# A four-layer hybrid decoder step: four row groups at once, squares summed in pairs, and operations moved

## The chip, the cores and the metric

The kernel runs on all 8 cores of one Trainium2 chip. Every core works on its own sequence of the prompt (2048 positions) and on 16 of the 128 samples; the cores exchange nothing. The metric is the device time of the slowest core in microseconds (us). The engines are named as in the profile: PE (TensorE, matmuls), DVE (VectorE), ACT (ScalarE), POOL (GpSimd; here it issues the weight loads), SP (SyncE; it issues all other DMAs).

## What is computed

Four layers with width 1024, then a final RMSNorm. The parts that the change touches:

```python
h = _rmsnorm(x, norm1_g)
zb, zc, zv, zu, ga, gs = jnp.split(h @ w_in, cuts, axis=-1)
conv_out, new_buf = _conv_causal(zc * zv, conv_buf, conv_w, conv_b)
ya = zb * conv_out
ys, hr, hi = _s5(zu, h0_re, h0_im, ...)      # diagonal complex state space
gy = jax.nn.gelu(ys, approximate=False)
ys = gy * jax.nn.sigmoid(gy @ w_glu + b_glu)
m = jax.nn.sigmoid(ga) * (ya @ w_branch[:512]) + jax.nn.sigmoid(gs) * (ys @ w_branch[512:])
x = x + m @ w_out
h2 = _rmsnorm(x, norm2_g)
gate, up = jnp.split(h2 @ w_gate_up, [D_FF], axis=-1)   # D_FF = 2816
x = x + (jax.nn.silu(gate) * up) @ w_down
```

RMSNorm divides by sqrt(mean(x*x) + 1e-6) over the 1024 channels. The state of the S5 part is h_t = A h_{t-1} + B u_t with 64 complex states for each group of 16 channels. Outputs are the normed prompt and samples, and the new convolution and S5 states.

## The kernel before

**Tiles.** X (fp32) holds the residual as 8 row tiles of 128 channels; H (bf16) the normed input, R (bf16) 16 row tiles of intermediate results. The sequence is done in two halves of 1024 positions, each through all four layers: half 0 in two blocks of 512 columns, half 1 in three blocks of 384, 384 and 272 columns (the last holds 256 positions and the 16 samples). Weights come through RING, 6 slots of 128x2048 bf16, loaded by POOL in the order of use; done_unit frees a slot and issues the next load.

**The mixer.** It projects zu into R (rows UT), then goes over f, the four row tiles of the S5 channels. For each f: stage_b (B u for 8 positions at a time: 64 matmuls of 32 rows x 128 weight columns x 128 columns, weights WBF), conv_proj (32 matmuls for zc and zv into CIN), stage_a (the part of the output within 8 positions, weights KF, 12 matmuls of up to 512 columns), scan (on DVE: turn the states by TW, two scans, turn back, write HBF), stage_d (the part from the carried states, weights CAF, 64 matmuls of 32 weight columns x 128 columns in four column groups) with two Gelus on ACT, conv_rest (the convolution on ACT and DVE, and 16 matmuls for zb). Stage_b runs as two groups hf, with row groups hf and hf+2 in each: row groups 0 and 1 share PSUM bank 0, and 2 and 3 bank 1. Stage_a and stage_d share banks 2 and 3. The projections of the mixer use banks 4 to 7. After the loop come sigmoid gates of the merge (up to five in advance), the glu, the merge, w_out and the FFN.

**The norm.** norm_block squares the eight row tiles on ACT into H; a matmul of each with ONESB sums over the channels in PSUM (eight, accumulated). Ln and Exp on ACT give the scale, and eight operations on DVE write H (or, in the final norm, SCR slots that SP stores to yp). In half 0 the final norm also issues, row tile by row tile, the loads of half 1's X; X for block 0 of half 1's first norm is loaded apart (HX, the "held" block). The samples' x is loaded (xs) after the final norm.

**The start.** params() computes A and related figures of all layers into AB on DVE and ACT, and sends part of it through a DRAM buffer chd, to have it back in another layout. prep_g makes WBF, TW, BXB, CAF and KF of a layer; for layers after the first it runs in steps beside the FFN of the layer before.

**The order.** Nothing is issued in program order. Sched collects all operations with what they read and write (keys such as ("ps", bank) or "FFN0", written in the FFN) and finalize lays out each engine's queue: a list planner that simulates the engines with a cost for each operation, takes the ready operation with the lowest priority number (position in the program plus a bias: EVICT first, LATER for what may come late), and adds 1900 ns for a DMA to land; loads over 400,000 bytes share a pipe of 230 bytes per ns. The queues are fixed then, and on the chip each engine works through its own strictly in order. The change alters the planner's figures, so the order may differ anywhere.

## Time and profile before

| | us |
|---|---|
| three runs: lowest / median / highest | 3686.79 / 3977.66 / 4197.6 |
| the profiled execution | 3685.78 |
| its span (first to last instruction, slowest core) | 3684.0 |
| the other cores' spans | 3677.5 to 3682.5 |
| PE busy in the span | 3531.0 (96%) |
| DVE busy | 1969.2 (53%) |
| ACT busy | 1194.1 (32%) |

The busy time is from the profiled execution on the slowest core. Matmuls overlap in the profile: the cost of a group of matmuls is read from its start to the start of what comes next, not from the durations. "Granted clock" is TensorE's clock as a share of 2.4 GHz; it is at 1.2 GHz or 2.4 GHz, and a value between the two is a mean over the stretch.

### The profile page before, as it was taken

The page shows a single profiled execution, that of the slowest core. Times are in us where ns is not written, and L with a number is a line of the kernel's source. Part 1 is how long each engine was busy: PE and PEld are TensorE (multiplying, and loading weights), DVE is VectorE, ACT ScalarE, POOL GpSimd, SP SyncE. Part 2 cuts the span into 40 slices and gives each one's busy share as a digit, 9 for nine tenths or more (in the row PEclk, how much of TensorE's full clock was granted, in tenths as well). Part 3 has the DMA queues.
Part 4 walks back from the last instruction along what each step waited for, and adds up shares of the span by engine and source line. Part 5 has one row for each costly group of instructions (what it writes and reads, how often), then busy time and mean ns, then how long its engine had stood idle before and what let it go on. Part 6 is the DMA issues. An engine that isn't in the chain of part 4 may idle for free.

```text
span 3684.0 us, 65802 instructions; the slowest of 8 cores (3677.5 to 3684.0 us)
## 1 busy us (share of the span) xinstructions
PE 3531.0 (96%) x23936; PEld 1970.0 (53%) x23936; DVE 1969.2 (53%) x3510; ACT 1194.1 (32%) x2263; POOL 274.5 (7%) x531
## 2 busy tenths in 40 slices
PE   4799999999999999999979999999999999999998
PEld 1444444444444444444446666666666666666665
DVE  5847337472555627365355572655627456374323
ACT  4424223341334323242233332334323342233212
POOL 1000000000000000000000000000000000000000
PEclk9899999999999999999989999999999999999999
DMA  5244444344444434354454343344434444333343
GB/s 115 49 75 70 78 71 78 69 75 70 75 78 81 75 64 72 71 99 76 74 130 78 69 83 65 64 88 73 75 64 70 82 74 77 58 73 70 68 79 80
DMA packets 99530, 279.51 MB, mean 76 GB/s; under 512 B 14352, under 2 KB 25488, under 8 KB 99216
## 3 DMA queue, kind: packets, MB, share of 16 engines
q0 software_dynamic: 72576, 243.30, 38.7%
q1 hardware_dynamic: 26640, 32.00, 2.8%
q8 instruction: 200, 3.28, 0.4%
q14 instruction: 114, 0.93, 0.1%
HBM read 508.55 MB, written 9.98 MB: 141 GB/s over the span
## 4 chain that ended last, share of the span: by engine, by line
PE 90%; DMA 3%; issue 2%; DVE 2%; ACT 2%; SPq 1%; DVEq 0%; ACTq 0%
PE ps L401 90%; DMA PRS<-chd 1%; ACT SCR L405 1%; DVE R L412 1%; DMA X<-xp 1%; DMA GS<-cst 0%; SPq L390 0%; ACT L405 0%; ACT R L405 0%; DMA R<-xp 0%; SPq L384 0%; DVE PRS L412 0%; DMA CIN<-xp 0%; DVE SCR L418 0%; DVE H L418 0%
## 5 line engine op out<-in xcount | busy, mean ns | idle before, releaser
L401 PE MATMUL ps<-H,RING 128*128 128x512 bf16 (+2 forms) x12160 | 2184.0, 339 | 49.9 <-ACT SCR L405 17.6
L401 PEld LDWEIGHTS ps<-H,RING 128*128 128x128 bf16 x12160 | 1181.1, 98 | 991.0 <-issue 83.3
L401 PE MATMUL ps<-R,RING 128*128 128x512 bf16 (+2 forms) x6400 | 1184.2, 338 | 4.9 <-ACT SCR L405 3.2
L405 ACT ACTIVATE SCR<-ps 128x384 f32<-128x384 f32 (+2 forms) x824 | 419.8, 514 | 1580.4 <-PE ps L401 1508.0
L401 PEld LDWEIGHTS ps<-R,RING 128*128 128x128 bf16 x6400 | 621.5, 98 | 495.4 <-issue 15.5
L412 DVE TENSOR_TENSOR R<-SCR,ps 128x272 bf16<-128x272 f32 (+2 forms) x520 | 296.2, 582 | 602.9 <-PE ps L401 563.6
L452 POOL DMA_DIRECT2D RING<-wseq x504 | 266.2, 528 | 3365.7 <-PE ps L401 3241.1
L412 DVE TENSOR_TENSOR X<-X,ps 128x512 f32<-128x512 f32 (+2 forms) x480 | 280.2, 584 | 406.3 <-PE ps L401 403.5
L412 DVE TENSOR_TENSOR SCR<-SCR,ps 128x512 f32<-128x512 f32 (+2 forms) x304 | 173.9, 581 | 261.2 <-PE ps L401 228.6
L405 ACT ACTIVATE H<-X 128x512 bf16<-128x512 f32 (+2 forms) x352 | 189.0, 543 | 287.1 <-DVE X L412 273.6
L412 DVE TENSOR_TENSOR PRS<-PRS 128x256 f32<-128x256 f32 (+2 forms) x391 | 194.0, 505 | 81.5 <-DMA PRS<-chd 56.9
L418 DVE SCALAR_TENSOR_TENSOR H<-X,PT,SCR 128x512 bf16<-128x512 f32 (+2 forms) x312 | 182.3, 644 | 25.5 <-ACT SCR L405 25.4
L401 PE MATMUL ps<-H,ONESB 128*128 128x384 bf16 (+2 forms) x360 | 117.0, 351 | 55.4 <-ACT H L405 53.5
L405 ACT ACT_TABLE_LOAD x67 | 86.0, 1283 | 138.7 <-PE ps L401 85.4
L405 ACT ACTIVATE R<-ps 128x512 bf16<-128x512 f32 (+5 forms) x164 | 79.1, 544 | 80.1 <-PE ps L401 79.8
L405 ACT ACTIVATE WBF<-PRS,MG 128x512 bf16<-128x512 f32 x128 | 92.1, 719 | 36.8 <-DVE PRS L412 32.2
L412 DVE TENSOR_TENSOR CIN<-ps,SCR 128x512 f32<-128x512 f32 (+2 forms) x80 | 46.7, 584 | 103.7 <-PE ps L401 103.7
L405 ACT ACTIVATE CAF<-PRS 64x512 bf16<-64x512 f32 x112 | 70.4, 629 | 97.8 <-DVE PRS L412 92.7
L412 DVE TENSOR_TENSOR R<-SCR 128x384 bf16<-128x384 f32 (+2 forms) x152 | 89.0, 586 | 14.0 <-DVE SCR L412 1.4
L401 PEld LDWEIGHTS ps<-H,ONESB 128*128 128x128 bf16 x360 | 34.3, 98 | 102.5 <-issue 83.7
L401 PE MATMUL ps<-R,WBF 32*128 32x128 bf16 (+1 forms) x2176 | 74.6, 217 | 14.7 <-DVE PRS L412 8.4
L412 DVE TENSOR_TENSOR PRS<-TW 128x16 f32<-128x16 f32 (+6 forms) x196 | 84.6, 460 | 7.6 <-issue 0.2
(90 smaller groups left out, 1266.6 us busy)
## 6 DMA issues: line engine op xcount, KB each, us to landing
RING<-wseq POOLq DMA_DIRECT2D x376, 512.0 KB, 6.1
RING<-wseq POOLq DMA_DIRECT2D x64, 384.0 KB, 4.8
RING<-wseq POOLq DMA_DIRECT2D x64, 320.0 KB, 4.1
X<-xp SPq DMA_DIRECT2D x8, 512.0 KB
PRS<-chd SPq DMA_DIRECT2D x32, 128.0 KB
yp<-SCR SPq DMA_DIRECT2D x16, 256.0 KB, 10.3
yp<-SCR SPq DMA_DIRECT2D x16, 192.0 KB, 2.0
GS<-bst SPq DMA_DIRECT2D x8, 256.0 KB
```

The lines of the kernel that those rows point to most:

```text
L401: return S.op("pe", lambda e: e.matmul(out, lhsT=lhsT, rhs=rhs, start=start, stop=stop, **kw), reads=reads, writes=writes, mode=pmode(lhsT ...
L405: return S.op("act", lambda e: e.activation(out=out, in_=in_, func=func, **kw), reads=reads, writes=writes, cost=180.0 + 0.83 * numel(out) ...
L412: return vop(lambda e: e.tensor_tensor(out=out, in0=a, in1=b, op=op), out, reads, writes, bias)
L418: return vop(lambda e: e.scalar_tensor_tensor(out=out, in0=a, scalar=s, in1=b, op0=op0, op1=op1), out, reads, writes, bias, 1.1)
L452: S.op("pool", lambda e: e.dma_start(out=RING[:, slot, 0:n], in_=wseq[l, :, o:o + n]), writes=[("w", slot)], deps=deps, dma_sem=f"w{slot}" ...
```

## The change

- Half 0: stage_b4 takes the place of stage_b, with all four row groups in one group of 64 matmuls, each row group in a bank of its own (banks 0 to 3, columns 0 to 255).
- Half 0: stage_y takes the place of stage_a and stage_d. It uses columns 256 to 511 of banks 0 to 3, and runs one tile later: stage_y(f-1) after scan(f), stage_y(3) at the end.
- Half 0, all norms but the first of layer 0 and the final one: the squares of row tiles 0 and 1, 2 and 3, 4 and 5 go to SCR in fp32, DVE adds the two into H, and PE sums five tiles.
- The final norm of half 0: the stores of a block come after all its loads of X; the second block's results go to R and not to SCR.
- x_sample is loaded at the start into unused columns of X, and copied by ACT where it was loaded before. The last loads of X (384 columns) wait for the norm of half 1's last block.
- The negation of C in prep_g waits for AB; the copies and products of sample_loads wait for FFN0. The first layer's KF uses banks 6 and 7.
- The planner: a DMA lands after 3500 ns, loads over 100,000 bytes share a pipe of 260 bytes per ns; tiled matmuls cost 0.108 ns a column (0.216 with two row groups at work).

```diff
+NPAIR = (0, 2, 4)
...
-                if o.nbytes > 400000:
-                    pipe = max(pipe, end) + o.nbytes / 230.0
+                if o.nbytes > 100000:
+                    pipe = max(pipe, end) + o.nbytes / 260.0
                     end = pipe
-                end += 1900.0
+                end += 3500.0
...
-        cost = max(26.0, n * 0.23) if "tile_position" in kw else max(36.0, n / 2.4 + 1.0)
+        cost = max(7.0, n * (0.216 if two else 0.108)) if "tile_position" in kw else max(36.0, n / 2.4 + 1.0)
...
-        ts(stc[:, 1, :], stc[:, 1, :], -1.0, None, ALU.mult, ALU.bypass, kC + ["FFN0"], kC)
+        ts(stc[:, 1, :], stc[:, 1, :], -1.0, None, ALU.mult, ALU.bypass, kC + ["FFN0", "AB"], kC)
...
-            b = 2 + f % 2 if PF["first"] else 7
+            b = 6 + f % 2 if PF["first"] else 7
...
-        act(SSTB[:], SST[:], AF.Copy, ["SST"], ["SSTB"])
+        act(SSTB[:], SST[:], AF.Copy, ["SST", "FFN0"], ["SSTB"])
...
+        pairs = NPAIR if out_h and held is None and not st["xh"] and gidx0 + (gname == "n2") else ()
...
-            act(H[:, kt, sq:sq + n], xk[kt][0], AF.Square, xk[kt][1] + fgk, gk("H", kt, sq, n))
-            mm(PS[:, b, 0:n], ONESB[:], H[:, kt, sq:sq + n], kt == 0, kt == 7, gk("H", kt, sq, n) + ["ONESB"], [("ps", b)], 0, EVICT)
+            hk = gk("H", kt, sq, n)
+            if kt in pairs:
+                i, j = scr(), scr()
+                act(SCR[:, i, 0:n], xk[kt][0], AF.Square, xk[kt][1] + fgk, sk(i))
+                act(SCR[:, j, 0:n], xk[kt + 1][0], AF.Square, xk[kt + 1][1] + fgk, sk(j))
+                tt(H[:, kt, sq:sq + n], SCR[:, i, 0:n], SCR[:, j, 0:n], ALU.add, sk(i) + sk(j), hk)
+            elif kt - 1 in pairs:
+                continue
+            else:
+                act(H[:, kt, sq:sq + n], xk[kt][0], AF.Square, xk[kt][1] + fgk, hk)
+            mm(PS[:, b, 0:n], ONESB[:], H[:, kt, sq:sq + n], kt == 0, kt == 7, hk + ["ONESB"], [("ps", b)], 0, EVICT)
...
+            if half == 0 and c0:
+                ov, ok = R[:, kt, :].bitcast(F32), gk("R", kt, 0, NCOL)
...
+        for kt, ov, ok in outs:
+            store(yp[0, :, kt, c0:c0 + n], ov[:, 0:n], ok + ["FGY"])
...
+        def stage_b4(f):
+            S.group()
+            for s in range(T):
+                m = T - 1 - s
+                for ri in range(2):
+                    for rg in range(4):
+                        h = slice(32 * rg, 32 * rg + 32)
+                        mm(PS[:, rg, 128 * ri:128 * ri + 128], WBF[h, m, ri, f, :], R[h, UT + f, s * 128:(s + 1) * 128],
+                           s == 0 and ri == 0, s == T - 1, ["WBF", ("R", UT + f, s)], [("ps", rg)],
+                           tile_position=(32 * rg, 0), skip_group_check=True)
+            S.endgroup()
...
+        def stage_y(f):
+            hb = f % 2
+            for b in range(4):
+                S.group()
+                for tau in range(T):
+                    j0 = max(2 * b, tau)
+                    if j0 > 2 * b + 1:
+                        continue
+                    nn = (2 * b + 2 - j0) * 128
+                    mm(PS[:, b, 256 + (j0 - 2 * b) * 128:512], KF[:, f, tau, :], R[:, UT + f, (j0 - tau) * 128:(j0 - tau) * 128 + nn],
+                       tau == 0, False, [("KF", f)] + gk("R", UT + f, (j0 - tau) * 128, nn), [("ps", b)], skip_group_check=True)
+                S.endgroup()
+            for b in range(4):
+                S.group()
+                for j in range(2):
+                    for ri in range(2):
+                        for rg in range(4):
+                            mm(PS[32 * rg:32 * rg + 32, b, 256 + j * 128:384 + j * 128], CAF[:, ri, 2 * b + j + 1, 4 * f + rg, :], HBF[:, hb, ri, rg, 0:128],
+                               False, j == 1 and ri == 1, ["CAF", ("HBF", hb)], [("ps", b)], tile_position=(0, 32 * rg), skip_group_check=True)
+                S.endgroup()
+            for bi in range(2):
+                act(R[:, YS + f, 512 * bi:512 * bi + 512].rearrange("p (b c) -> p b c", b=2), PS[:, 2 * bi:2 * bi + 2, 256:512], AF.Gelu,
+                    [("ps", 2 * bi), ("ps", 2 * bi + 1)], gk("R", YS + f, 512 * bi, 512))
...
-            stage_b(f)
+            (stage_b4 if four else stage_b)(f)
...
-            stage_a(f)
+            if not four:
+                stage_a(f)
             scan(f)
-            stage_d(f)
+            if not four:
+                stage_d(f)
+            elif f:
+                stage_y(f - 1)
             conv_rest(wbz, f)
...
+        if four:
+            stage_y(3)
...
+    load(X[:, :, 1024:1040], xs[:, :, :], [("X", kt, 5) for kt in range(8)])
...
-            load(X[:, :, 640:656], xs[:, :, :], [("X", kt, 3) for kt in range(8)])
+            act(X[:, :, 640:656], X[:, :, 1024:1040], AF.Copy, [("X", kt, 5) for kt in range(8)], [("X", kt, 3) for kt in range(8)])
...
-                load(X[:, kt, 656:1040], xp[1, :, kt, 0:384], xseg(kt, 656, 384))
+                load(X[:, kt, 656:1040], xp[1, :, kt, 0:384], xseg(kt, 656, 384), reads=gk("H", 7, *blocks(1)[2]))
```

## Rows read from the trace of the kernel before

**Rows 1.** The page: busy time of the engines, and two of the costliest groups.
```profile
PE 3531.0 (96%) x23936; PEld 1970.0 (53%) x23936; DVE 1969.2 (53%) x3510; ACT 1194.1 (32%) x2263; POOL 274.5 (7%) x531
...
L412 DVE TENSOR_TENSOR X<-X,ps 128x512 f32<-128x512 f32 (+2 forms) x480 | 280.2, 584 | 406.3 <-PE ps L401 403.5
```

**Rows 2.** Table of stages: length, busy us of PE, PEld, DVE, ACT, POOL, clock, DMA share, GB/s.
```profile
0.00:151.00 151.00, 77.77 (x609) 37.25 (x610) 105.83 (x216) 64.58 (x118) 14.71 (x39) 0.85 0.39 81
...
562.17:577.87 15.70, 15.70 (x189) 8.18 (x188) 14.68 (x19) 6.64 (x11) 1.06 (x2) 1.00 0.38 69
...
1470.00:1487.00 17.00, 10.43 (x106) 4.92 (x107) 2.54 (x6) 7.20 (x12) 0.53 (x1) 0.95 0.46 104
...
1830.00:1874.00 44.00, 18.18 (x73) 7.08 (x71) 17.51 (x27) 13.24 (x30) 1.58 (x3) 0.66 0.92 242
1890.00:3450.00 1560.00, 1532.31 (x12288) 1005.08 (x12285) 880.57 (x1696) 538.19 (x1109) 111.92 (x212) 1.00 0.41 72
3450.00:3684.00 234.00, 219.79 (x1499) 146.09 (x1496) 67.33 (x133) 43.37 (x94) 16.89 (x32) 0.98 0.43 80
```

**Rows 3.** Time line of PE in a mixer of half 0: start, us, operation, [idle before].
```profile
542.53 1.07 PE L401 MATMUL ps<-R,WBF 32*128 32x128 bf16 x32
543.53 1.58 PE L401 MATMUL ps<-R,KF 128*128 128x512 bf16 x8
...
562.17 1.09 PE L401 MATMUL ps<-HBF,CAF 128*32 128x128 bf16 x64
563.20 1.90 PE L401 MATMUL ps<-H,RING 128*128 128x512 bf16 x8
564.99 2.11 PE L401 MATMUL ps<-R,KF 128*128 128x512 bf16 x12
566.94 1.89 PE L401 MATMUL ps<-H,RING 128*128 128x512 bf16 x8
```

**Rows 4.** Time lines of DVE and ACT at the start.
```profile
28.11 0.29 DVE L415 TENSOR_SCALAR GS<-GS 128x256 f32<-128x256 f32 x1 [15.30 <-DMA GS<-cst]
...
58.06 1.29 DVE L412 TENSOR_TENSOR PRS<-PRS 128x512 f32<-128x512 f32 x2 [7.82 <-DMA PRS<-chd]
...
28.55 0.63 ACT L405 ACTIVATE CAF<-GS 64x512 bf16<-64x512 f32 x1 [13.87 <-DVE PRS L418]
```

**Rows 5.** Time line of ACT in the mixer of layer 3, half 0.
```profile
1483.82 0.63 ACT L405 ACTIVATE SSTB<-SST 128x512 bf16<-128x512 f32 x1 [6.93 <-DMA SST<-sst]
1484.46 1.28 ACT L405 ACT_TABLE_LOAD   x1
```

**Rows 6.** Time lines of DVE and ACT at the turn between the halves.
```profile
1848.25 0.75 DVE L418 SCALAR_TENSOR_TENSOR SCR<-X,PT,SCR 128x512 f32<-128x512 f32 x1 [8.35 <-DMA yp<-SCR]
...
1869.99 0.20 ACT L405 ACTIVATE EPSC<-EPSC 128x1 f32<-128x1 f32 x1 [8.26 <-DMA X<-xs]
```

**Rows 7.** Time line of PE: matmuls of the samples on WBF, half 1.
```profile
3301.21 0.36 PE L401 MATMUL ps<-R,WBF 32*128 32x16 bf16 x16
3301.49 1.47 PE L401 MATMUL ps<-H,RING 128*128 128x384 bf16 x8
```

**Rows 8.** Time line of PE from the last stage_d of a mixer to the glu, half 0.
```profile
608.09 1.10 PE L401 MATMUL ps<-HBF,CAF 128*32 128x128 bf16 x64
609.12 10.53 PE L401 MATMUL ps<-H,RING 128*128 128x512 bf16 x48
619.49 15.70 PE L401 MATMUL ps<-R,RING 128*128 128x512 bf16 x72
```

**Rows 9.** Time line of ACT in the same stretch: the last two Gelus.
```profile
608.93 1.28 ACT L405 ACT_TABLE_LOAD   x1
610.22 1.08 ACT L405 ACTIVATE R<-ps 128x512 bf16<-128x512 f32 x2
```

**Rows 10.** Time line of PE with one matmul of a norm among those of w_down.
```profile
1822.81 0.38 PE L401 MATMUL ps<-H,ONESB 128*128 128x512 bf16 x1
1823.02 2.32 PE L401 MATMUL ps<-R,RING 128*128 128x512 bf16 x10
```

**Rows 11.** Time line of POOL at the start.
```profile
34.42 0.53 POOL L452 DMA_DIRECT2D RING<-wseq  x1 [9.37 <-DMA X<-xp]
```

41 lines of the change are left out of this document (24 added, 17 removed).

## The prediction

> **What bounds the kernel now.** First the page's busy shares [rows 1]: the matrix engine (PE) is busy 3531.0 of 3684.0 us, so a change can save PE work, or the 153 us in which PE is idle. Second the table of stages [rows 2], for where the idle time lies: 73.2 us in the first 151 us (151.00 less 77.77), 6.6 in the 17 us around 1480, 25.8 in the 44 us of the turn from half 0 to half 1, 27.7 in 1560 us of half 1 and 14.2 in the last stage. In a mixer of half 0 there is none in 15.70 us [rows 2]. So in the layers of half 0 only removed PE work counts, and at three places only removed waits. Third the time line of PE in that mixer [rows 3]: what a stage of the state space costs is the start of what follows it less its own start. Fourth the time lines of the other engines at the three idle places [rows 4 to 6]: what each waited for.
>
> **Four row groups (half 0: 4 layers x 4 tiles f = 16 stages).** Before, stage_b is two groups of 32 matmuls; one takes 1.00 us (542.53 to 543.53) [rows 3], 31 ns a matmul, two at work at a time. Stage_b4 issues the same 64 in one group, four at a time, in four banks. No row shows four row groups; the nearest is stage_d, 64 matmuls of 128 columns in four column groups: 1.03 us (562.17 to 563.20), 16.1 ns each [rows 3]. Its weights are narrower (32 columns and not 128), so I look for a bound by weight loads: 16 matmuls of 16 columns on the same 128-column weights, two row groups, take 0.28 us from start to start [rows 7], 17.5 ns each with the change of mode in it. So the load of the weights allows 17.5 ns or less, and the new stage is 1.03 us, at most 64 x 17.5 = 1.12. It saves 2.00 - 1.03 = 0.97; bounds 0.88 and, if four groups go exactly twice as fast, 1.00. If the banks or the weight path let only two run, it saves 0. 0.97 x 16 = 15.5 us; but in the first two stages PE waits for other engines anyway, so 13.6.
>
> Small tiled matmuls follow each other at 16.1 and 17.5 ns here [rows 3, 7]. The Trainium skill (TensorE: Matmul & The Clock Gate, section "Wait — 56ns, not 53.3ns?") gives a floor of about 25 ns between starts however small the matmul is. By it 64 would take an estimated 1.6 us, and the edit would give 0.4 x 16 = 6 us. The trace contradicts it, so it isn't used.
>
> **Stage_y for stage_a and stage_d.** The KF part goes from 12 matmuls of up to 512 columns to 20 of up to 256, with 4608 columns either way. The 12 take 1.95 us (564.99 to 566.94) [rows 3]; 4608 columns at 2.4 GHz are 1.92, which leaves 2.5 ns for each. Eight more cost 0.02 us a stage, or 0.15 if weight loads show: 0.3 us in all, up to 2.4. The CAF part keeps its 64 at 1.03 us.
>
> What changes more is order. Banks 0 to 3 now hold both B (columns 0 to 255) and Y (256 to 511), and are tracked whole. So stage_b4(f+1) waits for the Gelu of f-1, that for stage_y(f-1), and that for scan(f) to have read the banks. Queued behind a late stage_b4 are scan(f+1) on DVE and at last the glu. Per f PE now has 15.70 - 0.97 = 14.7 us of work, and DVE 14.68 [rows 2]: level. PE doesn't wait while it has gate matmuls to fill with. Before, the last stage_d starts at 608.09, and PE reaches the glu at 619.49 after 48 gate matmuls [rows 8]. With 4 x 0.97 = 3.9 us less work PE would reach it at 615.6. The last tile needs stage_y(3) behind scan(3): 608.1 + 3.0 (1.95 + 1.03), then a table load and two Gelus, 1.28 + 1.08 [rows 9]: 613.5. The margin is 2.1 us, small but positive. I take 0.5 us lost a layer: 2 us; bounds 0 and 3.9 a layer.
>
> **Squares in pairs (norm_block, half 0).** Not touched are the first n1, the final norm, the held block and all of half 1. What remains is n2 in 4 layers and n1 in 3, two blocks each: 14 blocks x 3 = 42 matmuls of 512 columns. One of them moves the next matmul by 0.21 us (1822.81 to 1823.02) [rows 10], and PE is dense there: 8.8 us. Added are 3 additions a block on DVE, at 0.58 us as for X<-X,ps [rows 1]: 1.7 us a block. They lie beside FFN and w_out matmuls, where DVE is below its mean of 53% [rows 1]; where that cover is gone, the worst is 14 x 1.7 = 24 us. Tiles 6 and 7 stay single, so the end of the norm's chain gets no longer. ACT does the same eight squares.
>
> **The start.** DVE stands 15.30 us, to 28.11, before the negation in GS, which waits for the load of C, with params() queued behind it; ACT stands 13.87 us before the CAF copy that reads it, with the Ln of the first norm queued behind [rows 4]. The change ties the negation to AB, which params() writes: params() goes first, and the load lands meanwhile. Next late is the round trip through chd: DVE stands 7.82 us, to 58.06 [rows 4]. The planner reckoned 1.9 us a DMA; with 3.5, and a pipe from 100 KB on, it puts other work there. Then X: the ring unit that waits for the third chunk of X's block 1 issues at 34.42 [rows 11], so block 1 can't be normed before some 36, and the chd stores queue behind such loads. DVE is busy 105.83 of the 151 us [rows 2], densely from 60 on, so what it gains early it keeps. Bounds: 10 (part of the 15.3 goes to X and chd) and 15.3 + 7.8 = 23. I take 19, the 15.3 and half of the 7.8.
>
> **Around 1480.** ACT stands 6.93 us before the copy of SST, with the table load for the glu queued behind [rows 5]; PE's 6.6 us [rows 2] are that. The copy now needs FFN0, so it comes in the FFN, where ACT has room. 6.6 us, and 0.4 for the clock (0.95 in this stage): 7; bounds 3 and 9.
>
> **The turn between the halves.** PE is idle 25.8 of 44 us, with the granted clock at 0.66, so at 1.2 GHz for two thirds of it [rows 2]. Stores of the final norm and loads of X alternate on SP's queue; DVE stands 8.35 us for a free SCR slot, and the squares of block 2 start at 1869.99 after 8.26 us for the load of x_sample, which sits behind loads that nobody needs yet [rows 6]. After the change the stores of block 0 come behind its eight loads, block 1 is normed into R and waits for no slot, x_sample has been in X since the start, and the 384-column loads follow the norm of block 2. The stage moved 242 GB/s for 44 us [rows 2], 10.6 MB. Before block 2 there are still 2.6 MB of X, four ring units of 0.52 MB and the 2.1 MB of stores in between: 6.8 MB, 28 us at that rate, from 1828: 1856, against 1870, so 14 us. Block 1 has only 2.1 MB and the ring units ahead (17 us, 1845), so its 32 zu matmuls (384 columns at 2.4 GHz: 5.1 us) are done by then too. 14 + 5 = 19; bounds 10 and 24. The ACT copy that takes the place of the load is 128 elements: nothing.
>
> **The rest.** The planner's new figures also reorder half 1, where no step is edited. Its 27.7 us of idle time bound a gain; I take 0, and 5 either way. The last stage's 14.2 us stay.
>
> **Sum** against the profiled execution's own time, 3685.78 us (span 3684.0): 13.6 - 0.3 - 2 + 8.8 + 19 + 7 + 19 = 65.1, so **3621 us**. The profiled execution is within 0.03% of the lowest of the three runs shown (3686.79); their median, 3977.66, and highest, 4197.6, are 7.9% and 14% above, which no row explains. The forecast stands on the profiled time.
>
> **Rivals.**
> (A) The waits clear fully: start 23, 1480 9, turn 24, half 1 gives 5, and no new stall in the mixer. 13.6 + 8.8 + 23 + 9 + 24 + 5 = 83: 3602. For it: each wait has one cause that an edit takes away. Against: X isn't in before 36 us, whatever DVE does.
> (B) DVE becomes the bound of the mixer: the 2.1 us margin is missing (the gates run out early), and what PE saves there turns into a wait before the glu. 3621 + 13.6 - 2 = 3633. For it: 14.68 against 14.7 us.
> (C) It doesn't do what it says: only two row groups run at once (3621 + 13.6 = 3635), or the chd round trip takes over the wait of 15.3 (3621 + 15 = 3636). Against the first: [rows 7].
> (D) Slower than before: the ring b4(f), scan(f), y(f-1), Gelu, b4(f+1) through the shared banks becomes serial. If scan's reads of the banks stand behind the convolution's work on DVE (some 5 of the 14.68 us), and b4 behind the Gelus, one f takes 14.7 + 5 + 1.0 + 3.0 + 2.4 = 26 us and not 15.7. Gates cover 17 us a layer (80 matmuls of 512 columns). That costs 16 x 10.3 - 4 x 17 = 97 us: 3718. It decides from 24 us an f on, where the loss eats the whole gain of 65. Against: each f has 48 matmuls of conv_proj and conv_rest, 10.4 us, that use neither these banks nor HBF.
>
> **Chances.** Forecast 0.55 (3607 to 3633), A 0.22, B 0.09, C 0.10, D 0.04. The range takes in A with half 1's 5 us beyond it, B and C: 3596 to 3645. Faster by over 2% (about what a measurement of this kernel can tell from no change) is under 3612: most of A and a quarter of the forecast's own spread, 0.34. Slower by over 2% (over 3759) is the far end of D: 0.02. Within: 0.64.
>
> **What would show it.** In the profile after: on WBF one run of 64 matmuls in 1.03 us; 102 matmuls of 128x512 on ONESB where 144 were; no long wait of DVE on GS, and PE dense from about 132 and not 151; no wait on SST near 1480; the squares of the last block of the first norm of half 1 some 50 us earlier than 1870. It would be wrong if PE showed waits for ACT R or DVE PRS in the mixers of half 0, or if DVE stood for chd as long as it stood for GS.

## The result

| | us |
|---|---|
| the changed kernel, median of 4 runs (lowest to highest) | 3634.02 (3632.04 to 3684.15) |
| the kernel before, median of 4 runs on the same chip | 3833.61 (3686.79 to 4197.6) |
| ratio, 95% interval | 0.9851 (0.9823 to 0.988) |
| the profiled execution, its span | 3632.04, 3630.4 |

In some executions of a kernel the cores of one die get a lower clock; they are left out of the ratios (which is why this one isn't the quotient of the medians) and of the single times given for the experiments. The change makes the kernel 1.2 to 1.8% faster. Against the profiled execution before (span 3684.0) the gain is 53.6 us; the forecast was 65.1. The time, 3634, lies inside the range and 13 us above the forecast of 3621.

First the page of the changed kernel, the lines that answer to [rows 1]:

```profile
span 3630.4 us, 65960 instructions; the slowest of 8 cores (3623.5 to 3630.4 us)
...
PE 3501.4 (96%) x24022; PEld 1963.7 (54%) x24022; DVE 1991.1 (55%) x3552; ACT 1214.5 (33%) x2278; POOL 274.5 (8%) x531
...
L402 PE MATMUL ps<-H,ONESB 128*128 128x384 bf16 (+2 forms) x318 | 101.6, 347 | 44.9 <-ACT H L406 33.7
```

PE is busy 29.6 us less and idle 129.0 us instead of 153. On ONESB there are 318 matmuls where 360 were, and 102 of 512 columns where 144 were: the 42 of the forecast. Then the table of stages, against [rows 2] (same columns; the places are the same ones, moved by what was gained ahead of them):

```profile
0.00:151.00 151.00, 88.10 (x755) 40.90 (x756) 115.81 (x227) 68.95 (x126) 15.78 (x41) 0.88 0.43 89
...
1787.00:1831.00 44.00, 26.29 (x119) 12.45 (x117) 20.53 (x35) 14.27 (x33) 1.58 (x3) 0.69 0.86 222
```

PE is idle 62.9 us in the first 151 (73.2 before), and 17.7 in the 44 us of the turn (25.8 before).

**Where the time went, by stretch.** A stage can't be compared by its clock time once the ones ahead of it have moved. The trace gives a better ruler: every kernel here issues 18560 matmuls on RING in nearly the same order, so the start of the k-th can be compared. The table gives the us between some of them, as the median of the cores whose trace holds all 18560 (six of eight): to the first of layer 1 (k = 1856), to the first of layer 3 (5568), to the merge of layer 3 (6018), to the first of half 1 (7424), to the end of the turn (7574), and to the first of the last ten (18550), which the column "last matmul" gives.

| | start and layer 0 | layers 1, 2 | mixer 3 | rest of half 0 | turn | half 1 | last matmul |
|---|---|---|---|---|---|---|---|
| before | 523.3 | 865.2 | 129.3 | 316.0 | 61.2 | 1769.0 | 3664.0 |
| changed | 507.4 | 856.0 | 116.8 | 312.6 | 52.9 | 1767.1 | 3612.7 |
| gain | 15.9 | 9.2 | 12.5 | 3.4 | 8.3 | 1.9 | 51.3 |
| forecast | 22.9 | 11.8 | 10.4 | 1.3 | 19 | 0 | 65.1 |

(The forecast's terms by stretch: 19, 2 stages and 2 norm places; 8 stages and 4 norm places; 4 stages and 7; 1 norm place; 19; each mixer less the 0.5 for new waits. A stage is 0.97 us. A norm place, two blocks, is 8.8 / 7 = 1.26 us, and stage_y's 0.3 is left out.) So the turn is 10.7 us short, the start 7.0 and the layers 1 and 2 2.6; mixer 3 and the rest of half 0 are 2.1 better each. The 1.9 of half 1 is no more than the cores of one run differ by there (1766.6 to 1769.8 us in the changed kernel).

What the changed mixer looks like is in the time line of PE, against [rows 3]:

```profile
126.51 2.13 PE L402 MATMUL ps<-R,KF 128*128 128x256 bf16 x20
128.57 1.09 PE L402 MATMUL ps<-HBF,CAF 128*32 128x128 bf16 x64
129.60 3.63 PE L402 MATMUL ps<-H,RING 128*128 128x512 bf16 x16
133.16 1.07 PE L402 MATMUL ps<-R,WBF 32*128 32x128 bf16 x64
134.16 8.81 PE L402 MATMUL ps<-H,RING 128*128 128x512 bf16 x40
```

Stage_b4 takes 1.00 us (133.16 to 134.16) for its 64 matmuls, 15.6 ns each with four at work; the forecast was 1.03, and two groups took 2.00. KF's 20 take 2.06 and not 1.95.

Around the end of layer 0 there are waits of PE that the kernel before doesn't have at these places (same view):

```profile
506.80 3.61 PE L402 MATMUL ps<-H,RING 128*128 128x512 bf16 x16 [1.05 <-DVE X L413]
...
515.44 7.07 PE L402 MATMUL ps<-H,RING 128*128 128x512 bf16 x32 [0.92 <-DVE H L419]
523.34 1.07 PE L402 MATMUL ps<-R,WBF 32*128 32x128 bf16 x64 [0.84 <-ACT R L406]
```

### The profile page after: what moved, and what is told of

Read it like the earlier page. It is cut to its first block, busy times and chain, and to the rows that moved or that the text cites. A ratio compares the mean times of both kernels' runs of the same rounds, so it can differ in the third digit from the quotient of the medians.

```text
span 3630.4 us, 65960 instructions; the slowest of 8 cores (3623.5 to 3630.4 us)
## 1 busy us (share of the span) xinstructions
PE 3501.4 (96%) x24022; PEld 1963.7 (54%) x24022; DVE 1991.1 (55%) x3552; ACT 1214.5 (33%) x2278; POOL 274.5 (8%) x531
## 4 chain that ended last, share of the span: by engine, by line
PE 93%; issue 2%; DVE 2%; ACT 1%; DMA 1%; SPq 0%; DVEq 0%; ACTq 0%
PE ps L402 93%; DMA X<-xp 1%; ACT SCR L406 1%; ACT L406 0%; DVE PRS L413 0%; DVE H L419 0%; DMA yp<-SCR 0%; SPq L391 0%; DVE X L413 0%; DVE SCR L419 0%; ACT R L406 0%; DVE R L413 0%; ACT H L406 0%; DVE GS L912 0%; DVE HBF L413 0%
## 5 line engine op out<-in xcount | busy, mean ns | idle before, releaser
L402 PE MATMUL ps<-H,RING 128*128 128x512 bf16 (+2 forms) x12160 | 2180.4, 339 | 28.3 <-ACT SCR L406 11.8
L406 ACT ACTIVATE H<-X 128x384 bf16<-128x384 f32 (+2 forms) x268 | 137.2, 519 | 205.8 <-DVE X L413 184.5
L402 PE MATMUL ps<-H,ONESB 128*128 128x384 bf16 (+2 forms) x318 | 101.6, 347 | 44.9 <-ACT H L406 33.7
L413 DVE TENSOR_TENSOR R<-R,SCR 128x512 bf16<-128x512 bf16 (+2 forms) x80 | 45.7, 586 | 91.1 <-ACT SCR L406 90.5
L413 DVE TENSOR_TENSOR PRS<-ps,TW 128x1024 f32<-128x1024 f32 x64 | 76.0, 1218 | 24.7 <-PE ps L402 22.8
```

The source lines that it names most:

```text
L402: return S.op("pe", lambda e: e.matmul(out, lhsT=lhsT, rhs=rhs, start=start, stop=stop, **kw), reads=reads, writes=writes, mode=pmode(lhsT ...
L406: return S.op("act", lambda e: e.activation(out=out, in_=in_, func=func, **kw), reads=reads, writes=writes, cost=180.0 + 0.83 * numel(out) ...
L413: return vop(lambda e: e.tensor_tensor(out=out, in0=a, in1=b, op=op), out, reads, writes, bias)
```

## The experiments

Each kernel is the changed one with the edit shown, unless it says otherwise. The ratios are to the kernel before, on the same chip and in the same hour. Single cores scatter by some 5 us, most of it at the start, where X arrives, and at the turn, and some 3 us in half 1. From the 400th matmul to mixer 3 a stretch repeats within 0.1 us from core to core, and in mixer 3 and behind it within 0.2, except in the kernel before, where these two scatter by 3. So a difference of 1 or 2 us in the start, the turn or half 1 shows little.

**No pairs.**

```diff
-NPAIR = (0, 2, 4)
+NPAIR = ()
```

> The changed kernel with all eight squares summed by PE again (pairs off), the rest as it is. If the pairs are worth the PE work they remove, as I predicted, this kernel is 8.8 us slower than the changed kernel (3634 + 9 = 3643), and PE is dense around the norms in both. Rival: DVE stands before each addition (0.8 us for ACT in the time line of the changed kernel) and the additions of X come late, so that PE waits at the ends of the blocks; then the pairs are worth 3 us or less (3634 to 3637), and the waits of PE for DVE X and DVE H in half 0 (about 0.9 us each) are gone here.

Ratio 0.986 (0.9839 to 0.9881). On cores 1 to 3 the start and layer 0 take 508.9 us, layers 1 and 2 859.2, mixer 3 115.2, the rest of half 0 313.6. From the 400th matmul to the end of the FFN of layer 3 the pairs give 2.5 + 3.2 - 1.5 + 1.0 = 5.2 us, not 8.8. That lies between the theory and the rival. From the 400th matmul to the end of layer 0 the 2.5 us are the full 1.26 at each of two norm places, and then part is given back. The same place in the time line of this kernel shows how:

```profile
507.62 0.38 PE L402 MATMUL ps<-H,ONESB 128*128 128x512 bf16 x1
508.83 1.02 PE L402 MATMUL ps<-H,RING 128*128 128x512 bf16 x4 [0.83 <-DVE X L413]
509.69 0.38 PE L402 MATMUL ps<-H,ONESB 128*128 128x512 bf16 x1
509.91 13.30 PE L402 MATMUL ps<-H,RING 128*128 128x512 bf16 x60
```

With eight sums PE doesn't wait for H here; with five it comes to the first projections of block 1 0.92 us too early. The norm's chain (add to X, square, sum, Ln, Exp, eight products) has a length of its own, and PE work taken out in front of it turns into a wait. On core 1 this wait stands at the ends of layers 0 and 2 (0.92 and 1.08 us) and not at that of layer 1, so it is 2.0 of the 3.6 us that are missing; the rest lies in smaller steps. The wait for DVE X is there without pairs too, 0.83 us and not 1.05.

**Two row groups.**

```diff
-        four = half == 0
+        four = False
```

> The changed kernel with stage_b, stage_a and stage_d in half 0 as before (two row groups at a time, banks 0 and 1 apart from 2 and 3). If the four row groups give the 0.97 us a stage on the path, the first two stages aside, this is 13.6 us slower: 3634 + 14 = 3648, and 0.97 x 4 = 3.9 us a layer from one mixer to the next. Rival: DVE bounds the mixer, or the shared banks cost what PE saves; then under 2 us a layer, 3634 + 8 = 3642 or less.

Ratio 0.989 (0.985 to 0.9929); layers 1 and 2 take 861.3 us and not 856.0, mixer 3 120.5 and not 116.8, the start and layer 0 506.5 and not 507.4 (four cores). Each single mixer is 3.0 to 3.9 us longer, of the 3.9 expected, so the stage is worth what was forecast. But in the mixer of layer 0 the four row groups give nothing, and from the 400th matmul to the end of that layer they cost 1.2 us. Of the 7.8 us of layers 1 and 2 only 5.3 are left. With two row groups PE has no wait for DVE X in half 0; with four it has one of 0.93 us in the middle of layers 0 and 2, and one of 1.05 at their ends, and one for DVE H behind that. The rest goes to a wait in the mixer of layer 2, in the time line of PE in the changed kernel:

```profile
982.56 1.44 PE L402 MATMUL ps<-R,KF 128*128 128x256 bf16 x12 [1.22 <-DVE PRS L413]
```

In all 5.3 + 3.7 - 0.9 = 8.1 us, between the 13.6 of the theory and the 8 of the rival.

**The turn: the key FGY for each block.**

```diff
-                xk[kt][1] + ["PT"] + sk(i), ok + (["FGY"] if kt == 7 else []))
+                xk[kt][1] + ["PT"] + sk(i), ok + ([("FGY", c0)] if kt == 7 else []))
...
-            store(yp[0, :, kt, c0:c0 + n], ov[:, 0:n], ok + ["FGY"])
+            store(yp[0, :, kt, c0:c0 + n], ov[:, 0:n], ok + [("FGY", c0)])
```

> The changed kernel with the key FGY kept apart for the two blocks of half 0's final norm. As it is, the last scaling of block 1 (row tile 7) writes the key that the stores of block 0 read, so it waits until all of them have landed (1816.67 in the trace), and with it the last load of X, the copy of x_sample and the norm of half 1's last block. Theory: that false dependency is what is left of the turn; without it row tile 7 is scaled at about 1801 and the norm of the last block starts some 6 to 8 us earlier than 1818: 3634 - 7 = 3627. Rival: the DMA traffic of the stores in front of the loads bounds it (2.1 MB at some 240 GB/s, 9 us), and the start moves by under 2 us: 3632 to 3634.

Ratio 0.9853 (0.9837 to 0.9868), turn 55.4 us and not 52.9, and longer on every core (54.9 to 56.0; in the changed kernel 50.7 to 53.7). What the turn of the changed kernel looks like, in the time line of SP:

```profile
1795.48 10.55 SPq L391 DMA_DIRECT2D yp<-SCR  x8
1806.18 11.74 SPq L385 DMA_DIRECT2D X<-xp  x8
```

of ACT:

```profile
1817.51 0.31 ACT L406 ACTIVATE X<-X 128x128 f32<-128x128 f32 x1 [5.59 <-DVE R L419]
1817.91 0.20 ACT L406 ACTIVATE EPSC<-EPSC 128x1 f32<-128x1 f32 x1
1818.02 2.65 ACT L406 ACTIVATE H<-X 128x272 bf16<-128x272 f32 x8
```

and of PE:

```profile
1818.58 2.62 PE L402 MATMUL ps<-H,ONESB 128*128 128x272 bf16 x8 [8.00 <-ACT H L406]
1821.99 14.52 PE L402 MATMUL ps<-H,RING 128*128 128x384 bf16 x80 [0.79 <-ACT SCR L406]
```

The copy of x_sample stands 5.59 us for the last product into R. That product writes FGY, which the stores of block 0 read, so it waits for them. With the key split (ACT, same core) that wait is gone, and another stands there:

```profile
1804.79 0.31 ACT L406 ACTIVATE X<-X 128x128 f32<-128x128 f32 x1
1819.04 0.20 ACT L406 ACTIVATE EPSC<-EPSC 128x1 f32<-128x1 f32 x1 [13.94 <-DMA X<-xp]
```

and PE:

```profile
1819.71 4.14 PE L402 MATMUL ps<-H,ONESB 128*128 128x272 bf16 x11 [14.94 <-ACT H L406]
```

The products are done 13 us earlier, but the last loads of X go out behind the stores either way. Counted from the first load of X (1788.20 in the changed kernel, 1790.66 here), the squares of block 2 begin after 28.4 us where they began after 29.8: the key held them up by 1.4 us and not by 6 to 8. My theory fell: the key isn't what bounds this place. And the order changed with the key: ACT did six squares of block 1 from 1805.23 on in the changed kernel; here they stand behind the wait for block 2, though by the landing times in the trace their data were in by 1811.48. That is where the turn loses.

**The turn: the sums of half 1's blocks without priority.**

```diff
-hk + ["ONESB"], [("ps", b)], 0, EVICT)
+hk + ["ONESB"], [("ps", b)], 0, 0 if st["xh"] and gidx0 == 0 and out_h else EVICT)
```

> The changed kernel, but the norm sums of half 1's second and third block no longer go in front of all else in PE's queue. In the changed kernel the eight sums of the last block stand before the 32 zu matmuls of block 1, whose input is ready from 1812.8, and PE waits for ACT until 1818.58. Theory: with program order the zu matmuls of block 1 (5.1 us) run in that gap: 3634 - 5 = 3629. Rival: the planner puts them behind again, or the sums come later by as much as is gained: 3634.

Ratio 0.9863 (0.9831 to 0.9896), turn 51.3 us, which is inside the scatter; the eight sums of block 2 still stand ahead of block 1's zu. As I read finalize, the planner takes whatever it thinks ready, and asks for the priority only among those; that this decides here isn't shown. This says nothing of what the other order would give.

**The turn: all 16 stores behind all loads of X.**

```diff
-                outs.append((kt, ov, ok))
+                st.setdefault("outs", []).append((kt, c0, n, ov, ok))
...
-        for kt, ov, ok in outs:
-            store(yp[0, :, kt, c0:c0 + n], ov[:, 0:n], ok + ["FGY"])
+        if half == 0 and c0:
+            for kt, s0, sn, ov, ok in st["outs"]:
+                store(yp[0, :, kt, s0:s0 + sn], ov[:, 0:sn], ok + ["FGY"])
```

> The changed kernel, but at the turn the stores of block 0's final norm too are issued only after the loads of X for block 1 (all loads, then all sixteen stores). In the changed kernel the eight loads that half 1's last block needs are issued from 1806 to 1818, behind eight stores that take SP 10.6 us to issue. Theory: these stores are what is left at the turn; without them the loads issue by about 1801, the last block is squared at 1808 to 1810 and not 1818, and the kernel is 8 us faster (3626). Rival: the DMA engines are full with the ring's units and the first loads until some 1810 in any case, and the last block starts at 1815 or later: at most 3 us (3631).

There is no ratio for it; its lowest run took 3635.12 us, turn 53.9 us (from -3.3 to +4.6 by core). Counted from the first load of X (1784.41 here), the first squares of block 2 begin 12 us earlier than in the changed kernel and the others 6, and yet nothing comes of it (ACT, and below it PE, core 1):

```profile
1802.20 0.20 ACT L406 ACTIVATE EPSC<-EPSC 128x1 f32<-128x1 f32 x1 [4.04 <-DMA X<-xp]
...
1808.42 2.73 ACT L406 ACTIVATE H<-X 128x272 bf16<-128x272 f32 x7 [4.55 <-DMA X<-xp]
```

```profile
1802.86 1.62 PE L402 MATMUL ps<-H,ONESB 128*128 128x272 bf16 x4 [6.16 <-ACT H L406]
...
1815.02 15.74 PE L402 MATMUL ps<-H,RING 128*128 128x384 bf16 x88 [0.79 <-ACT SCR L406]
```

ACT stands twice for a chunk of block 2 while block 1's last four squares wait behind in its queue; their data landed by 1801.83. The queues were laid out for other times of arrival.

**The start: the transposes first, by priority.**

```diff
-mode=(128, 64, "f32"), cost=250.0)
+mode=(128, 64, "f32"), cost=250.0, bias=2 * EVICT)
```

> The changed kernel with params()'s four fp32 transposes put in front of the norm sums in PE's queue. In the changed kernel AB is copied by 27.4 but the transposes run at 33.36, behind two sums of block 1 that wait for the last chunk of X. Theory: the start was bounded there, at the round trip through chd; the transposes run at about 28, chd is back 5 us earlier, and as DVE bounds the start the kernel is 5 us faster (3629). Rival: the chd stores and loads queue behind X in the DMA engines until X is in, and nothing is gained before 36: 0 to 1 us (3633).

Ratio 0.9853 (0.9833 to 0.9872). The order didn't change, so the question stayed open for the key below.

**The start: the first layer's KF without priority.**

```diff
-["BXB", "CAF"], [("ps", b)], 0, EVICT, tile_position=(0, 32 * rg))
+["BXB", "CAF"], [("ps", b)], 0, 0 if PF["first"] else EVICT, tile_position=(0, 32 * rg))
```

> The changed kernel, but the first layer's KF matmuls no longer go in front of everything in PE's queue. In the changed kernel PE waits 28.57 us for CAF and does stage_b4(0) only at 102.66, after them, while WBF is ready at 93.9; DVE then stands 5.91 us before scan(0). Theory: with stage_b4(0) first DVE has scan(0) at about 96, and its 5.9 us go: 3634 - 5 = 3629. Rival: DVE is bound by its prep work and takes the KF work in that gap either way; 0 to 2 us.

Ratio 0.9849 (0.983 to 0.9869), again with the order unchanged.

**The start: the negation without AB.**

```diff
-ALU.bypass, kC + ["FFN0", "AB"], kC)
+ALU.bypass, kC + ["FFN0"], kC)
```

> The changed kernel without the new dependency of the negation of C on AB. If that edit is what moved params() ahead of the wait for the load of C, DVE stands some 10 to 15 us at GS again and the kernel is 9 to 15 us slower (3643 to 3649). Rival: the planner's new DMA figures alone (3500 ns, a pipe from 100 KB on) place the negation behind params(), and it makes no difference (3634).

Ratio 0.9849 (0.9832 to 0.9866): no difference. Params() comes first without that key too. The edit that the forecast took for the cause does nothing beside the planner's new figures; what it does with the old ones stands below.

**The planner's three figures for DMAs alone, on the kernel before.**

```diff
-                if o.nbytes > 400000:
-                    pipe = max(pipe, end) + o.nbytes / 230.0
+                if o.nbytes > 100000:
+                    pipe = max(pipe, end) + o.nbytes / 260.0
                     end = pipe
-                end += 1900.0
+                end += 3500.0
```

> The kernel before with nothing but the planner's three figures for DMAs (100,000 bytes, 260 bytes per ns, 3500 ns). Theory: the 12.5 us that the start gained come from these figures, because with them the planner puts params() before the negation and the CAF copy; so the start shows 10 to 14 us less than before, the wait at 1480 stays (no key keeps the copy of SST out of the mixer), the turn stays within 3 us (stores and loads still alternate), half 1 is within 3 us: in all 3672 to 3678 us, ratio 0.996 to 0.998. Rival 1, the start is gained by the AB key and the load of x_sample as well, each for a part: 0 to 6 us at the start, 3680 to 3690. Rival 2, the figures also cost the 2.7 us that half 1 lost in the changed kernel: it shows here as +2 to +4 us between the first and the last mixer of half 1.

The profiled run took 3660.57 us (the kernel before in the same hour 3687.78 to 3695.47); there is no ratio for it. By stretch: 502.9, 865.2, 120.2, 313.5, 63.6, 1771.1. The sum, 27.5 us, is half of the whole change, and above what I expected: 20.4 at the start, 9.1 in mixer 3, 2.5 in the rest of half 0, and 4.5 lost at the turn and in half 1. That the wait around 1480 would stay, as expected, was wrong. At the start DVE stands 1.56 us for the load of C and not at all for chd, where the kernel before stands 13.98 and 7.88 (core 1 of both). The wait for the load of SST went although no key keeps the copy out of the mixer: the planner, told that a DMA takes 3.5 us, put it behind the sigmoids of the merge (time line of ACT, against [rows 5]):

```profile
1467.67 0.69 ACT L405 ACTIVATE SCR<-ps,PT 128x512 f32<-128x512 f32 x1 [0.17 <-ACT SCR L405]
1468.25 0.62 ACT L405 ACTIVATE SSTB<-SST 128x512 bf16<-128x512 f32 x1
```

**The old three figures in the changed kernel** (the same lines, back).

> The changed kernel with the old three figures for DMAs. Theory 1, the AB key does the same at the start as the figures do (params() is forced ahead): start within 3 us of the changed kernel, turn the same (its order of transfers is set by keys), half 1 perhaps 2 to 3 us better: 3630 to 3636 us. Theory 2, the figures alone place the start's work well, and with the old ones the planner lets DVE and ACT stand for the loads of C or of chd: start 5 to 13 us worse, 3639 to 3647.

Ratio 0.9908 (0.9891 to 0.9924), 3655.33 us; by stretch 524.8, 855.8, 116.7, 312.5, 52.1, 1773.5. The start is 17.4 us worse, and half 1 6.4. Theory 1 fell, and theory 2 was too small. Mixer 3 stays at 116.7: with the old figures FFN0 alone removes that wait. The start shows what the AB key does by itself (DVE, core 1):

```profile
35.36 0.29 DVE L416 TENSOR_SCALAR GS<-GS 128x256 f32<-128x256 f32 x1 [2.64 <-DMA GS<-cst]
...
48.40 1.29 DVE L413 TENSOR_TENSOR PRS<-PRS 128x512 f32<-128x512 f32 x2 [10.50 <-DMA PRS<-chd]
```

The wait for the load of C is short, as the forecast had it, but the one for chd is now 10.50 us and not 7.82, and the start as a whole (524.8) is no better than before the change (523.3). That is the second half of rival C, in this kernel and not in the changed one.

**Without FFN0 in sample_loads.**

```diff
-        act(SSTB[:], SST[:], AF.Copy, ["SST", "FFN0"], ["SSTB"])
+        act(SSTB[:], SST[:], AF.Copy, ["SST"], ["SSTB"])
...
-            tt(t1, SST[:, ri], ar, ALU.mult, ["SST", "AB", "FFN0"], kk)
+            tt(t1, SST[:, ri], ar, ALU.mult, ["SST", "AB"], kk)
...
-        tt(SCVW[:], SCV[:, 1], w[1], ALU.mult, ["SCV", "PT", "FFN0"], ["SCVW"])
+        tt(SCVW[:], SCV[:, 1], w[1], ALU.mult, ["SCV", "PT"], ["SCVW"])
```

> The changed kernel without the key FFN0 at the copy of SST and at the two products of sample_loads; all queues stay the same up to layer 3 of half 0, where the copy of SST goes back into the mixer, 25 or so operations of ACT ahead. Theory: the wait before the glu comes back and with it 7 to 9.5 us, all of it between the mixer of layer 3 of half 0 and its glu: 3641 to 3644 us, ratio 0.987 to 0.989. Rival: with the stages shorter the load of SST lands in time in any case, or the loss is filled by other gates: 0 to 2 us, 3634 to 3636. Second rival: the key costs half 1 something (the copy of SST stands late among the FFN's operations); then half 1 is 1 to 3 us better without it.

Ratio 0.9845 (0.9826 to 0.9865); mixer 3 116.8 us, no loss at all. The rival was right: the copy stands at 1463.52 behind the sigmoids and waits for nothing. With the run before: the key and the figures each remove the same wait, and one of them is enough.

**The transposes first, by a key.**

```diff
-writes=[("ps", b)], mode=(128, 64, "f32"), cost=250.0)
+writes=[("ps", b), "TRP"], mode=(128, 64, "f32"), cost=250.0)
...
-hk + ["ONESB"], [("ps", b)], 0, EVICT)
+hk + ["ONESB"] + (["TRP"] if PF["first"] and c0 and kt >= 4 else []), [("ps", b)], 0, EVICT)
```

> The changed kernel with one dependency more: the last four sums of block 1 of the first norm read a key that the four transposes of params() write, so that PE does the transposes about 5 us earlier (their input is ready at 27.4 us, and they start at 33.4). Only this place in PE's queue changes. Theory: the round trip through chd, which starts with them, bounds the start: 3 to 5 us less at the first WBF matmul and after, 3629 to 3631 us, ratio 0.9838 to 0.9845. Rival, the loads of X and of the weights bound the start, or DVE is busy without a gap from 33 us on: 0 to 1 us, 3633 to 3635.

Ratio 0.9842 (0.9827 to 0.9856), 3631.8 us; start and layer 0 505.9 us. It lies between theory and rival, near the scatter. On core 1 DVE waits 0.23 us for the transposes where it waited 6.15, and then 3.64 for the load of C, where it hadn't waited. The key was tried twice more below.

**The old cost of tiled matmuls.**

```diff
-        cost = max(7.0, n * (0.216 if two else 0.108)) if "tile_position" in kw else max(36.0, n / 2.4 + 1.0)
+        cost = max(26.0, n * 0.23) if "tile_position" in kw else max(36.0, n / 2.4 + 1.0)
```

> The changed kernel with the planner's old cost for tiled matmuls (26 ns at least, 0.23 ns a column). The order of the first matmuls stays; in the mixers fewer projections are put ahead of the state space's matmuls (40 and not 56, 24 and not 40), and the rest for the glu. Theory: the new costs are part of the worse start (the planner holds PE for free earlier than it is); with the old ones the start up to the glu of layer 0 gains 2 to 5 us, the mixers of layers 1 to 3 stay: 3629 to 3632 us. Rival: the old costs overstate stage_b4 (64 x 29.4 ns = 1.88 us against 1.01 measured), and the projections run out before the last stage_y: each mixer of half 0 costs 0.5 to 2 us more: 3636 to 3642.

Ratio 0.9867 (0.9853 to 0.9881), 3640.55 us: 1.8 us worse at the start, 1.2 in mixer 3, 1.6 in half 1. The rival was right in the time; costs near the measured ones help. Of these three only the 1.2 is clear of the scatter.

**KF in bank 7 alone.**

```diff
-            b = 6 + f % 2 if PF["first"] else 7
+            b = 7
```

> The changed kernel with the first layer's KF in bank 7 alone and not in 6 and 7 (banks 2 and 3, as before, would meet the scan's reads of stage_b4's banks). With the planner's new figures alone the glu of layer 0 started at 164.5 us in the median, in the changed kernel near 171, although four of its stages are 0.97 us shorter. Theory: KF has taken two of the four banks of the projections; PE does 120 projection matmuls before it stands for the first CAF copy, where 136 were done with the figures alone. With bank 6 free 8 more come before that wait (108 and not 100 in the last run of them), and the layer ends 1.5 to 4 us earlier: 3630 to 3632.5. Rival: KF's own copies are the chain (PE stood 2.36 us for one), and one bank instead of two makes it longer, by a copy and its latency three times: 0 to 3 us slower, 3634 to 3637.

Ratio 0.9857 (0.9841 to 0.9873), 3636.5 us; start and layer 0 511.6. The rival was right: one bank less for KF costs what one more for the projections gives, and more. The wait for CAF falls from 28.57 to 27.14 us, but KF's last group now starts 10.1 us behind the first and not 7.5, and on every core PE then meets a wait that the changed kernel doesn't have (core 1):

```profile
124.04 4.00 PE L402 MATMUL ps<-R,KF 128*128 128x256 bf16 x20 [4.44 <-DVE PRS L413]
```

The twenty matmuls behind it take 4.00 us and not 2.13, at a granted clock of 0.50.

**The last edit and the key TRP together.**

> Both edits of the start together: KF in bank 7 alone, and the transposes ahead of the last four sums of block 1. Theory: the two add (2 us, and 1.5 to 4): 3628 to 3631 us, the fastest of all kernels here, ratio 0.983 to 0.9845. Rival: both only move the wait to DVE's work on the first layer's weights, and X's arrival sets the rest: 3632 to 3635.

Ratio 0.9852 (0.9836 to 0.9867), 3633.8 us: not the fastest, since one half of it loses. Against the kernel with bank 7 alone the key is worth 5.4 us at the start and 2.6 at the last matmul.

**The figures alone and KF in banks 6 and 7**, on the kernel before.

```diff
-            b = 2 + f % 2 if PF["first"] else 7
+            b = 6 + f % 2 if PF["first"] else 7
```

> The kernel before with the planner's three figures for DMAs (as the earlier run of the figures alone) and one edit more: the first layer's KF in banks 6 and 7. In PE's queue the projections ahead of the first KF matmuls drop from 120 to 96 in their last run. Theory: this edit is what the changed kernel lost at the start; the 24 matmuls (5.2 us) come after the wait for CAF and not in it, so the end of layer 0 comes 4 to 9 us later than with the figures alone (464.4 us from the first projection to the second layer's first, median of the cores), 3664 to 3669 us. Rival: PE stands for CAF only to stand less later; 0 to 2 us, 3660 to 3662.

Ratio 0.9908 (0.9873 to 0.9942). By stretch 507.5, 865.2, 120.2, 313.6, 64.8, 1768.6: the start and layer 0 cost 4.6 us more than with the figures alone, as the theory says at its low end, and all the rest repeats, but for the turn and half 1. The device time doesn't show all of it (3661.62 us). Side by side, PE at the start on a core where both reach it at the same time: with the figures alone (core 3, KF in banks 2 and 3)

```profile
57.31 12.25 PE L401 MATMUL ps<-H,RING 128*128 128x512 bf16 x56 [0.84 <-ACT R L405]
92.92 1.05 PE L401 MATMUL ps<-CAF,BXB 128*32 128x256 bf16 x16 [23.36 <-ACT CAF L405]
```

and here (core 3, KF in banks 6 and 7):

```profile
57.32 7.07 PE L401 MATMUL ps<-H,RING 128*128 128x512 bf16 x32 [0.84 <-ACT R L405]
92.94 1.04 PE L401 MATMUL ps<-CAF,BXB 128*32 128x256 bf16 x16 [28.55 <-ACT CAF L405]
```

CAF is ready at the same time, but with two of its four banks given to KF PE runs out of projections 24 matmuls or 5.2 us earlier, and they come after the wait. The two waits are 23.36 and 28.53 to 28.55 us on every core looked at. The changed kernel has the long one (core 1):

```profile
94.63 1.04 PE L402 MATMUL ps<-CAF,BXB 128*32 128x256 bf16 x16 [28.57 <-ACT CAF L406]
...
98.58 3.59 PE L402 MATMUL ps<-H,RING 128*128 128x512 bf16 x8
102.11 0.62 PE L402 MATMUL ps<-CAF,BXB 128*32 128x256 bf16 x8
```

The eight projections right behind it take 3.5 us from start to start where eight take 1.8 elsewhere: the granted clock is 0.50 from 94.6 to 102.1 and 1.00 from 104.3 on. All kernels here pay that, with either wait.

**Layer 0 as before.**

```diff
-            b = 6 + f % 2 if PF["first"] else 7
+            b = 2 + f % 2 if PF["first"] else 7
...
-        four = half == 0
+        four = half == 0 and l > 0
```

> The changed kernel with layer 0 of half 0 as before (two row groups, stage_a and stage_d, KF in banks 2 and 3); layers 1 to 3 keep four row groups. It gives up 4 x 0.97 = 3.9 us of PE work in layer 0 and has 16 projections more ahead of the wait for CAF (116 and not 100). Theory: the start gains 8 to 9 us by the freed banks and loses 3.9: 4 to 5 us net, 3628 to 3631 us, ratio 0.983 to 0.984. Rival: DVE bounds the first layer and the banks don't matter: 2 to 4 us slower, 3636 to 3638.

Ratio 0.9824 (0.9785 to 0.9863), 3636.14 us. By stretch 503.7, 855.8, 117.3, 314.5, 49.9, 1769.2: 3.7 us better at the start, 2.3 at the last matmul, but not in the device time, which should have been 3628 to 3631. The theory is right in the place; its sum isn't seen in the device time.

**The same, with TRP.**

> As the run with layer 0 as before, and the transposes ahead of the last four sums of block 1. Theory: 1 to 2 us less again, as the key gave alone (median of the cores 3610.4 against 3612.7 at the last matmul): 3626 to 3629 us, the fastest of all kernels here. Rival: the two take the same wait: as the run without the key, within 1 us.

Ratio 0.9811 (0.9772 to 0.985), four runs from 3626.08 to 3634.64 us. By stretch 499.4, 855.8, 117.3, 314.5, 50.0, 1767.0, the last matmul at 3604.0, 8.7 us ahead of the changed kernel's. The key gives 4.3 us at the start here, 1.5 alone and 5.4 beside bank 7, each time ahead, but no two alike and each within the scatter of single cores. So the wait for the transposes seems to bound the start for some us; how many, and whether by the round trip through chd, isn't shown. This kernel is the fastest by the median of the cores; by the device time it leads the changed kernel by some 4 us, which the intervals don't separate.

## Why the prediction was right or wrong

The sum was 65.1 us and 53.6 came. The largest part of what is missing, 10.7 us, lies at the turn, where 19 were forecast: the step that failed there is that the forecast reckoned only when data arrive and not what stands ahead in the queues. The start's 19 lacks a price for the move of KF (4.6 us), and the pairs' 8.8 came to 5.2. The edits that the forecast named as causes of the gain at the start and around 1480 weren't the causes. That the time is only 13 us off is partly luck: mixer 3 and the rest of half 0 gave 2.1 us more than forecast each, and half 1 shows 1.9, which together hide 6.1 of the 20.3 that the other stretches are short.

**Four row groups: the stage right, the sum too high.** The stage takes 1.00 us, forecast 1.03. Of the 13.6 less 2 us, 8.1 came. The mixers of layers 1 to 3 gave 3.0 to 3.9 each, so the 0.5 a layer for new waits there is about right. The step that failed is "in the first two stages PE waits for other engines anyway, so 13.6": all four stages of layer 0 gave nothing. The forecast also had no term for waits outside the mixers; the new ones for DVE X and DVE H at the norms of layers 0 and 2 take most of the rest. Stage_y was put at 0.3 us in all, and the KF part alone takes 0.11 a stage, 1.8 in all, inside the bound of 2.4.

**Pairs: mis-sized.** 8.8 became 5.2. "PE is dense there" was the step that failed. Dense is only what the time line showed with eight sums; three fewer laid bare the latency of the norm's chain, 0.92 and 1.08 us at two of the seven places. No run separates the cost of the additions on DVE; it is inside these 5.2.

**The start: mechanism partly wrong, sum too high.** 20.4 us come from the planner's DMA figures alone, which remove both the wait for C and the one for chd, and beside them the AB key adds nothing; the forecast had named the key as the cause and the figures for chd alone. Against them, the move of KF to banks 6 and 7 costs 4.6. The forecast listed that edit and never priced it: that is the step that failed. The pairs gave 1.5 in this stretch (508.9 less 507.4), the row groups took 0.9 (507.4 less 506.5), and the new cost of tiled matmuls gave 1.8: 20.4 - 4.6 + 1.5 - 0.9 + 1.8 = 18.2, against 15.9 measured. The three small terms are within the scatter, so the 2.3 left over says nothing.

**Around 1480: right in size, wrong in cause.** Figures alone 9.1 in mixer 3, and 2.5 behind it; with the row groups 12.5. FFN0 does it too with the old figures (116.7), so it wasn't needed beside the new ones.

**The turn: wrong, 19 against 8.3.** In both kernels the sums of block 2 follow the start of the last ten w_down matmuls, before by 38.1 us (1832.52 to 1870.66), now by 28.7 (1789.87 to 1818.58): 9.4 of the 14. (Put into the time of the kernel before, the squares of block 2 begin at 1861 and not at 1856.) The byte sum held: from the first load of X to these squares it gave 28 us, and 29.8 came, or 28.4 with the key FGY split. But that load goes out at 1788.20, which is 1831 in the time of before and not 1828; and the false dependency through FGY, which the forecast didn't see, costs the other 1.4. The other 5, for block 1's zu, didn't come at all. The products of block 1 begin on DVE at 1812.10, and its zu stood behind the eight sums of block 2 until 1821.99. The failed step is that I summed bytes and asked when data land, and not what stands ahead in the in-order queues of PE and ACT. Of three edits at this place one left the order as it was, one let data in 6 to 12 us earlier and gained nothing, and one lost 2.5 us; in the last two the queue held block 1's squares behind a wait for block 2. What a queue laid out for the real times would give wasn't tried.

**Half 1: 0 forecast, 1.9 measured, inside the 5 and inside the scatter.** The old figures cost it 6.4 in the changed kernel, so the order there is worth some us; the 2.1 that the new ones seem to cost in the kernel before aren't clear of the scatter.

**The rivals.** A, B and D didn't come; of the ring of banks the wait of 1.22 us above and one of 0.49 behind it are all that shows in the mixers of layers 1 to 3. The forecast had called a wait for DVE PRS there, or for ACT R, a sign that it was wrong: the first is this one, and the second stands 0.84 us ahead of the first WBF matmuls of layers 1 to 3, but with two row groups too. C's row groups did double, and chd took the wait over only with the planner's old figures. The time fell near B's 3633 by other causes.

## What to carry to other kernels

Where queues are laid out by a planner, first run the kernel before with the new cost figures alone: here they were half of the gain (27.5 of 51.3 us), and two hand-made dependencies did nothing beside them. Price each resource that a moved operation takes (two PSUM banks out of four cost 4.6 us), not only the operations. Work that is taken out in front of a chain of latency counts only up to the cover that the chain needs, and data that land early count only if the in-order queue has their reader next.

## What the runs showed of the hardware

Four row groups of 32 rows run at once, each in a bank of its own: 64 matmuls of 128 weight columns x 128 columns in 1.00 us, 15.6 ns each, exactly twice as fast as two groups (31 ns, [rows 3]). Twenty KF matmuls of up to 256 columns take 2.06 us where twelve of up to 512 with the same 4608 columns take 1.95: 0.11 us for eight more, 14 ns each. After the wait of 28.57 us at the start, eight matmuls of 512 columns took 3.5 us from start to start and not 1.8, and the granted clock stood at 0.50 until 102.1, 7.5 us behind the wait's end: an idle stretch is paid once more behind its end.
